# Second mixer's input projection: every weight block in the 512-column form, halves joined by ScalarE and VectorE

## Chip, cores and metric

The kernel runs on one core of one Trainium2 chip. The metric is the device time of one execution in microseconds (us), here the median of three runs.

## What is computed

A trunk of two layers over 256 tokens of width 2048, all in float32. Layer 0 mixes tokens with a gated linear recurrence, layer 1 with a state-space mixer (Mamba-2 SSD). Both layers then have a SwiGLU block and a gated per-layer embedding. The change lies in layer 1's mixer, cut here to its core:

```python
def ssd_mixer(u, w_in, conv_w, conv_b, dt_bias, a_log, d_skip, norm_g, w_out):
    zxbcdt = u @ w_in                       # 2048 -> 4096 (z) + 6144 (x, B, C) + 64 (dt)
    xbc = silu(causal_dwconv(xbc, conv_w, conv_b))      # 4 taps along the tokens
    xs, Bm, Cm = ...                        # 64 heads of 64; 8 groups share B and C of 128
    dt = softplus(dt + dt_bias)
    y = ssd_scan(xs, dt, -exp(a_log), Bm, Cm) + d_skip * xs
    y = y * silu(z)
    return (rmsnorm_per_group(y) * norm_g) @ w_out
```

## The kernel before

Activations lie transposed, 128 channels by 256 tokens a tile. To get float32 accuracy from a rounded format, each weight block and each activation tile is split into a high part (rounded) and a low part (the rest). A product of a 128x128 weight block is high x high + high x low + low x high. There are two forms of it (`piece`, lines 405 to 422). The three-matmul form (lines 401 to 403) adds all three products of 256 columns onto one half of a PSUM bank. The 512-column form does high weight x (high and low activations) in one matmul of 512 columns over the whole bank (line 419), then low weight x high activations over its first half (line 421). The result is then the sum of the two halves, which somebody has to add. `WIDE` (line 55) names the phases that use the 512-column form.

Weights come in pieces of eight blocks (512 KB) through a ring of four. SyncE loads piece p+4 when VectorE has finished the low part of piece p (`w_lo`). ScalarE rounds a landed piece to its high part (line 631, `w_hi`) when TensorE has used up the piece four before (`w_used`), VectorE subtracts to get the low part (line 925, `w_lo`), TensorE waits for `w_lo`. In their streams, ScalarE and VectorE handle piece q+3 first in step q, then the other work of step q.

The input projection of the mixer is phase B1. It runs in two halves of four head groups; between and after them comes the output projection B2. A head group makes ten output tiles from 20 pieces, two pieces a tile, in banks 2, 3, 0, 1 in turn: tiles 0 to 5 (B, C and four x tiles) go through the convolution, tiles 6 to 9 are z. Steps 0 to 11 use the three-matmul form and steps 12 to 19 the other, since z tiles are multiplied for a SiLU only. In odd steps VectorE waits for the piece and empties the bank: `bank x rinv` into `cpad` (line 1325), or for z tiles a reduce over both halves (`fold`, line 1123) and a multiply by half of rinv (line 1331). In even steps ScalarE does the tap of weight 3 with the bias (line 859), VectorE the other three (`later_taps`, lines 1133 and 1135), each waiting for the one before, ScalarE the Tanh of the tile before (line 866) and VectorE its SiLU (line 1318). Tile 5's Tanh and SiLU come in step 13.

After piece 14 TensorE needs all six SiLUs (`silu_done`): it multiplies B with C (line 568, 572) and transposes the x tiles (line 576). State products follow after piece 16 (line 582), outputs after pieces 17 and 19 (lines 594, 596). ScalarE makes the decay factors with Relu and Exp (lines 883, 887) in steps 11, 13, 15 and 17. Steps 0 to 8 also finish the head group before: its y on VectorE in step 0, a statistics matmul after piece 4 (line 603), variance and reciprocal in step 5 (lines 1390, 1391), the norm in step 7 (line 1396). In the very first head group there is none before, but the decay sums of all heads are computed in these steps (`decay_steps`), and their rows are read back by a DMA on SyncE's queue ahead of later weight loads. 

Of the kernel before, what the change touches and what calls it, by code (L numbers as in the profile page):

```python
# [54 lines left out]
WIDE = ("A2", "F1", "F2", "B2")  # L55
# [67 lines left out]
def trunk(nc, t, out):  # L123
    with ExitStack() as ctx:
# [73 lines left out]
        wdt = scratch(HEADS)  # L198

# [43 lines left out]
        eb_in, carry_mm, y_done_state = sem("eb_in"), sem("carry_mm"), sem("y_done_state")  # L243
        turned, xdec_done = sem("turned"), sem("xdec_done")
# [154 lines left out]
        def _(pe):  # L399
# [5 lines left out]
            def piece(ph, it, q, blocks):  # L405
# [3 lines left out]
                for b, (before, dst, src, k, first, last) in enumerate(blocks):  # L409
# [4 lines left out]
                    if ph["name"] not in WIDE and not (ph["name"] == "B1" and q >= 12 or gate):  # L414
                        mm = three(dst[:, 0:SEQ], whi[:, q % RING, cols], wlo[:, q % RING, cols], src[:, 0, k, :],
                                   src[:, 1, k, :], first, last)
                        continue
# [201 lines left out]
        def _(act):  # L619
# [38 lines left out]
            for index, ph in enumerate(phases):  # L658
# [97 lines left out]
                def body(it, first, ph=ph, name=name, n=n, index=index):  # L756
                    last = isinstance(it, int) and it == ph["iters"] - 1
                    for q in range(n):
# [84 lines left out]
                        if name == "B1":  # L843
                            group = it + ph["half"] * 4
                            very_first = first and ph["half"] == 0
                            if very_first:
# [70 lines left out]
        def _(dve):  # L917
# [139 lines left out]
            for index, ph in enumerate(phases):  # L1057
# [110 lines left out]
                def body(it, first, ph=ph, name=name, n=n, index=index):  # L1168
                    last = isinstance(it, int) and it == ph["iters"] - 1
                    for q in range(n):  # L1170
                        p = it * n + ph["piece0"] + q
                        w = width_of(index, ph, q, last)
                        if w and not (first and index == 0 and q == 0):
# [122 lines left out]
                        if name == "B1":  # L1296
# [12 lines left out]
                            if q % 2 == 0 and 2 <= q <= 12:  # L1309
                                nt = q // 2 - 1  # L1310
                                dve.wait_ge(tap_done, group * 6 + nt + 1)
                                later_taps(cpad[:, nt % 2], ca[:, nt, :],
                                           lambda k, nt=nt, group=group: flat(bpar[:, at(group), nt * 5 + k:nt * 5 + k + 1]),
                                           conv_done)
                            if q % 2 == 0 and 4 <= q <= 12 or q == 13:
                                nt = (q + 1) // 2 - 2
                                dve.wait_ge(conv_t, group * 6 + nt + 1)
                                V.scalar_tensor_tensor(out=ca[:, nt, :], in0=cth[:, nt % 2, :], scalar=1.0,
                                                       in1=ca[:, nt, :], op0=ALU.add, op1=ALU.mult).then_inc(silu_done, 1)
                            if q % 2 == 1:  # L1320
                                dve.wait_ge(w_used, p + 1)
                                src = bank[BANKS4[q // 2 % 4]][:, 0:SEQ]
                            if q % 2 == 1 and q < 12:
                                nt = q // 2
                                V.tensor_tensor(cpad[:, nt % 2, 3:3 + SEQ], src, rinv[:], ALU.mult).then_inc(bank_free, 1)
# [269 lines left out]
```

## Time and profile before

| | |
|---|---|
| median of 3 runs | 2690.71 us |
| lowest, highest | 2690.18, 2691.59 us |
| profiled execution | 2691.32 us |
| its span, first to last instruction | 2689.6 us |
| mean granted TensorE clock | 0.998 |
| TensorE busy | 99% |
| VectorE busy | 75% |
| ScalarE busy | 51% |
| GpSimd busy | 11% |

Shares are of the span. A busy TensorE isn't one at its peak, since matmuls overlap; the time from one start to another counts. Phase B1 lies between 1152 and 1412 us (first half) and between 1502 and 1751 us (second half), B2 behind each.

### The profile page before, as it was taken

To read this page: it belongs to the slowest core of one execution; us is meant where nothing else is said; L and a number is where in the kernel's file an instruction comes from. 1 tells how busy PE (TensorE), PEld (TensorE's weight loads), DVE (VectorE), ACT (ScalarE), POOL (GpSimd) and SP (SyncE) were. 2 spreads that over 40 slices of the span, in tenths; PEclk is the share of its full clock that TensorE was granted. 3 is DMA by queue.
4 is the path that set the end of the run, shared out by engine and by line. 5 is a ranking of instruction groups with operands and counts; after the bars stand their busy time and mean duration, and the time that the engine had idled before them with its cause. 6 is when DMAs were issued, how large, how long until landed. Compare 5 with 4: busy or idle time off the path is not lost.

```text
span 2689.6 us, 47811 instructions
## 1 busy us (share of the span) xinstructions
PE 2665.1 (99%) x16831; PEld 2400.6 (89%) x16831; DVE 2004.4 (75%) x2805; ACT 1377.1 (51%) x1869; POOL 284.9 (11%) x314
## 2 busy tenths in 40 slices
PE   9999999999999999999999999999999999999998
PEld 8999888888888888899998999988888888888887
DVE  7788776665666677889996799978666556667776
ACT  6776444444444445556664566644444444444454
POOL 1001300000000111100001000032000000001211
PEclk9999999999999999999999999999999999999999
DMA  6545565556655566655555555555555665555664
GB/s 217 179 173 193 178 199 187 188 174 189 206 189 188 192 189 197 191 178 185 190 185 187 202 183 188 188 186 189 187 189 179 184 206 190 191 189 173 188 202 137
DMA packets 154237, 504.62 MB, mean 188 GB/s; under 512 B 17104, under 2 KB 21520, under 8 KB 152976
## 3 DMA queue, kind: packets, MB, share of 16 engines
q1 hardware_dynamic: 154048, 503.14, 57.8%
q8 instruction: 64, 1.05, 0.2%
q14 instruction: 45, 0.37, 0.0%
q10 hardware_dynamic: 80, 0.07, 0.0%
HBM read 500.97 MB, written 2.16 MB: 187 GB/s over the span
## 4 chain that ended last, share of the span: by engine, by line
PE 95%; DVE 3%; ACT 1%; DMA 1%; issue 1%; SPq 0%; DVEq 0%; ACTq 0%
PE bank L419 51%; PE bank L421 26%; PE bank L401 5%; PE bank L403 5%; PE bank L402 5%; DVE wlo L925 1%; ACT whi L631 0%; PE bank L594 0%; DMA wraw<-in_A 0%; PE bank L576 0%; PE bank L582 0%; PE bank L596 0%; DMA wraw<-in_B 0%; DVE arena L1133 0%; DVE rinvh L979 0%
## 5 line engine op out<-in xcount | busy, mean ns | idle before, releaser
L419 PE MATMUL bank<-R,whi 128*128 128x512 f32 x5984 | 2089.0, 393 | 0.1
L421 PE MATMUL bank<-R,wlo 128*128 128x256 f32 x5984 | 1675.1, 280 | 0.0
L925 DVE TENSOR_TENSOR wlo<-wraw,whi 128x1024 fp32r<-128x1024 f32 (+2 forms) x1008 | 1166.5, 1164 | 545.8 <-ACT whi L631 544.0
L631 ACT ACTIVATE whi<-wraw 128x1024 fp32r<-128x1024 f32 (+2 forms) x1008 | 984.3, 983 | 917.6 <-PE bank L421 831.1
L419 PEld LDWEIGHTS bank<-R,whi 128*128 128x128 f32 x5984 | 1121.0, 187 | 252.5 <-issue 1.7
L421 PEld LDWEIGHTS bank<-R,wlo 128*128 128x128 f32 x5984 | 1130.8, 189 | 0.1
L401 PE MATMUL bank<-R,whi 128*128 128x256 f32 x1376 | 393.0, 286 | 5.1 <-DVE wlo L925 5.0
L403 PE MATMUL bank<-R,wlo 128*128 128x256 f32 x1376 | 389.5, 283 | 0.0
L402 PE MATMUL bank<-R,whi 128*128 128x256 f32 x1376 | 389.3, 283 | 0.0
L401 PEld LDWEIGHTS bank<-R,whi 128*128 128x128 f32 x1376 | 262.4, 191 | 9.6 <-DVE wlo L925 4.9
L402 PEld LDWEIGHTS bank<-R,whi 128*128 128x128 f32 x1376 | 262.5, 191 | 0.2
L403 PEld LDWEIGHTS bank<-R,wlo 128*128 128x128 f32 x1376 | 262.5, 191 | 0.0
L1123 DVE TENSOR_REDUCE arena<-bank 128x256 f32<-128x512 f32 x238 | 164.1, 690 | 57.5 <-PE bank L421 55.3
L1455 POOL TENSOR_TENSOR R<-arena,R 128x256 f32 x88 | 76.9, 874 | 1145.4 <-ACT R L830 1145.4
L830 ACT ACTIVATE R<-arena 128x256 f32 (+1 forms) x88 | 36.8, 418 | 187.1 <-DVE arena L1276 187.1
L1436 POOL TENSOR_TENSOR square<-h 128x256 f32 (+1 forms) x65 | 43.6, 670 | 485.8 <-DVE h L1249 481.3
L1437 POOL TENSOR_TENSOR sumsq<-sumsq,square 128x256 f32<-128x256 f32 x65 | 72.5, 1115 | 5.1
L1133 DVE SCALAR_TENSOR_TENSOR arena<-arena,bpar 128x256 f32<-128x256 f32 x96 | 53.2, 554 | 9.3 <-ACT arena L859 4.9
L1463 POOL TENSOR_TENSOR arena<-arena 128x512 f32<-128x512 f32 x8 | 10.9, 1364 | 454.0 <-ACT arena L898 454.0
L1248 DVE TENSOR_TENSOR h<-bank,h 128x256 f32<-128x256 f32 (+1 forms) x112 | 47.3, 423 | 8.6 <-PE bank L421 8.0
L1249 DVE TENSOR_TENSOR h<-bank,h 128x256 f32<-128x256 f32 (+1 forms) x112 | 47.6, 425 | 3.9
L971 DVE SCALAR_TENSOR_TENSOR R<-h,gains,R 128x256 fp32r<-128x256 f32 (+1 forms) x80 | 46.6, 582 | 3.2 <-DVE R L961 2.5
(177 smaller groups left out, 1274.9 us busy)
## 6 DMA issues: line engine op xcount, KB each, us to landing
wraw<-in_F SPq DMA_DIRECT2D x352, 512.0 KB, 3.3
wraw<-in_B SPq DMA_DIRECT2D x224, 512.0 KB, 3.3
wraw<-in_A SPq DMA_DIRECT2D x96, 512.0 KB, 3.6
wraw<-in_F SPq DMA_DIRECT2D x128, 384.0 KB, 3.1
wraw<-in_F SPq DMA_DIRECT2D x128, 320.0 KB, 3.2
wraw<-in_PL SPq DMA_DIRECT2D x64, 512.0 KB, 3.7
arena<-cs_rows SPq DMA_DIRECT2D x8, 1024.0 KB, 5.5
arena<-in_gates SPq DMA_DIRECT2D x8, 512.0 KB, 3.7
```

Source lines behind the costliest of these rows:

```text
L401: nc.tensor.matmul(dst, hi_w, hi_x, start=first, stop=False)
L402: nc.tensor.matmul(dst, hi_w, lo_x, start=False, stop=False)
L403: return nc.tensor.matmul(dst, lo_w, hi_x, start=False, stop=last)
L419: nc.tensor.matmul(dst.rearrange("p (s t) -> p s t", s=2), whi[:, q % RING, cols], src[:, :, k, :], start=first, stop=False)
L421: mm = nc.tensor.matmul(dst[:, 0:SEQ], wlo[:, q % RING, cols], src[:, 0, k, :], start=False, stop=last)
L631: nc.scalar.activation(whi[:, slot, 0:w * BLOCK], wraw[:, slot, 0:w * BLOCK], ACT.Copy).then_inc(w_hi, 1)
L925: V.tensor_tensor(wlo[:, slot, 0:w * BLOCK], wraw[:, slot, 0:w * BLOCK], whi[:, slot, 0:w * BLOCK].bitcast(F32), ALU.subtract).then_inc(w_ ...
L1123: own.link(V.tensor_reduce(dst, bank[number][:].rearrange("p (s t) -> p t s", s=2), mybir.AxisListType.X, ALU.add))
L1133: own.link(V.scalar_tensor_tensor(out=dst, in0=pad[:, k:k + SEQ], scalar=taps(k), in1=dst, op0=ALU.mult, op1=ALU.add))
L1249: V.tensor_tensor(row, src[:, SEQ:2 * SEQ], row, ALU.add).then_inc(bank_free, 1)
L1437: G.tensor_tensor(sumsq[:], sumsq[:], square[:], ALU.add).then_inc(sumsq_done, 1)
L1455: G.tensor_tensor(flat(dst[:, 1, at(it * 2 + j), :]), swi_u[:, j, :], flat(dst[:, 0, at(it * 2 + j), :]).bitcast(F32), ALU.subtract).then_ ...
```

## The change

`"B1"` joins `WIDE`, so that all 20 pieces of a head group use the 512-column form. In each odd step ScalarE copies the second half of the bank into a new two-buffer tile `low_half` (`half_done`), and VectorE adds it to the first half into the tile's place, then multiplies in place by rinv (or half of it) and frees the bank. The reduce isn't used in B1 any more. The taps are spread: in an even step VectorE does taps 2 and 1 of a tile with the SiLU of the tile before between them; its last tap comes in the next odd step, between the add and the multiply of the next tile. Tile 5's SiLU moves from step 13 to the very start of step 14, ahead of the weights' low part; its Tanh stays in step 13. VectorE's own count per head group goes from 26 to 32.

```diff
--- before.py
+++ after.py
@@ -52,7 +52,7 @@
 LAST_HEAD = {0: (0, 1), 1: (2, 3), 2: (4,), 3: (5,), 4: (6,), 5: (7,)}
 
 
-WIDE = ("A2", "F1", "F2", "B2")
+WIDE = ("A2", "B1", "F1", "F2", "B2")
 LAST = ((0, 4), (4, 4), (8, 4), (12, 2), (14, 2))
 GELU_C = 0.7978845608028654
 GELU_S = 0.044715 ** 0.5
@@ -196,6 +196,7 @@
         cst = scratch(2 * HEADS).rearrange("p (c e) -> p c e", c=2)
         dtt = scratch(2 * HEADS).rearrange("p (c e) -> p c e", c=2)
         wdt = scratch(HEADS)
+        low_half = scratch(2 * SEQ).rearrange("p (n t) -> p n t", n=2)
 
         dt_x, dt_e, dt_w, dt_z = [xtok[0:HEADS, c, n * SEQ:(n + 1) * SEQ] for c in range(2) for n in range(2)]
         dt_r, dt_v, dt_cs, dt_one = [zt[0:HEADS, n, :] for n in range(4)]
@@ -241,6 +242,7 @@
         tap_done, conv_done, conv_t, silu_done = sem("tap_done"), sem("conv_done"), sem("conv_t"), sem("silu_done")
         z_t, ebc_done, exp_done, sc_done = sem("z_t"), sem("ebc_done"), sem("exp_done"), sem("sc_done")
         eb_in, carry_mm, y_done_state = sem("eb_in"), sem("carry_mm"), sem("y_done_state")
+        half_done = sem("half_done")
         turned, xdec_done = sem("turned"), sem("xdec_done")
         y_mm, y_read, ysq_done, gstat_mm, gvar_done, grinv_done = (sem("y_mm"), sem("y_read"), sem("ysq_done"),
                                                                    sem("gstat_mm"), sem("gvar_done"), sem("grinv_done"))
@@ -411,7 +413,7 @@
                         pe.wait_ge(s, v)
                     cols = slice(b * BLOCK, (b + 1) * BLOCK)
                     gate = ph["name"] == "PL" and k < KT and not (q > 37 or q == 37 and b > 1)
-                    if ph["name"] not in WIDE and not (ph["name"] == "B1" and q >= 12 or gate):
+                    if ph["name"] not in WIDE and not gate:
                         mm = three(dst[:, 0:SEQ], whi[:, q % RING, cols], wlo[:, q % RING, cols], src[:, 0, k, :],
                                    src[:, 1, k, :], first, last)
                         continue
@@ -843,6 +845,11 @@
                         if name == "B1":
                             group = it + ph["half"] * 4
                             very_first = first and ph["half"] == 0
+                            if q % 2 == 1:
+                                act.wait_ge(w_used, p + 1)
+                                act.wait_ge(bank_free, it * 10 + ph["group0"] + 4 + q // 2 - 1)
+                                nc.scalar.activation(low_half[:, q // 2 % 2, :], bank[BANKS4[q // 2 % 4]][:, SEQ:2 * SEQ],
+                                                     ACT.Copy).then_inc(half_done, 1)
                             if very_first:
                                 decay_steps(q)
                             if q == 0 and not first:
@@ -1170,6 +1177,8 @@
                     for q in range(n):
                         p = it * n + ph["piece0"] + q
                         w = width_of(index, ph, q, last)
+                        if name == "B1" and q == 14:
+                            conv_silu(it + ph["half"] * 4, 5)
                         if w and not (first and index == 0 and q == 0):
                             lo(p + LEAD, q + LEAD, w)
                         g0 = it * ph["groups"] + ph["group0"] + 4
@@ -1309,26 +1318,24 @@
                             if q % 2 == 0 and 2 <= q <= 12:
                                 nt = q // 2 - 1
                                 dve.wait_ge(tap_done, group * 6 + nt + 1)
-                                later_taps(cpad[:, nt % 2], ca[:, nt, :],
-                                           lambda k, nt=nt, group=group: flat(bpar[:, at(group), nt * 5 + k:nt * 5 + k + 1]),
-                                           conv_done)
-                            if q % 2 == 0 and 4 <= q <= 12 or q == 13:
-                                nt = (q + 1) // 2 - 2
-                                dve.wait_ge(conv_t, group * 6 + nt + 1)
-                                V.scalar_tensor_tensor(out=ca[:, nt, :], in0=cth[:, nt % 2, :], scalar=1.0,
-                                                       in1=ca[:, nt, :], op0=ALU.add, op1=ALU.mult).then_inc(silu_done, 1)
+                                second = tap(group, nt, 2)
+                                if nt:
+                                    conv_silu(group, nt - 1)
+                                own.need(second)
+                                third = tap(group, nt, 1)
                             if q % 2 == 1:
-                                dve.wait_ge(w_used, p + 1)
-                                src = bank[BANKS4[q // 2 % 4]][:, 0:SEQ]
-                            if q % 2 == 1 and q < 12:
-                                nt = q // 2
-                                V.tensor_tensor(cpad[:, nt % 2, 3:3 + SEQ], src, rinv[:], ALU.mult).then_inc(bank_free, 1)
-                            if q % 2 == 1 and q > 12:
-                                j = q // 2 - 6
-                                if j == 0 and not very_first:
+                                tile = q // 2
+                                dst = cpad[:, tile % 2, 3:3 + SEQ] if tile < 6 else zt[:, tile - 6, :]
+                                dve.wait_ge(half_done, group * 10 + tile + 1)
+                                if tile == 6 and not very_first:
                                     dve.wait_ge(yn_lo, group * 4)
-                                fold(BANKS4[q // 2 % 4], zt[:, j, :])
-                                V.tensor_tensor(zt[:, j, :], zt[:, j, :], rinvh[:], ALU.mult).then_inc(bank_free, 1)
+                                folded = own.mark(V.tensor_tensor(dst, bank[BANKS4[tile % 4]][:, 0:SEQ], low_half[:, tile % 2, :],
+                                                                  ALU.add))
+                                if 1 <= tile <= 6:
+                                    own.need(third)
+                                    last_tap(group, tile - 1)
+                                own.need(folded)
+                                V.tensor_tensor(dst, dst, rinv[:] if tile < 6 else rinvh[:], ALU.mult).then_inc(bank_free, 1)
                             if q in (14, 16, 18):
                                 z_silu(group, q // 2 - 7)
                             if q == 18:
@@ -1365,6 +1372,23 @@
                                                 cbm.rearrange("p c l -> p (c l)").rearrange("p (e n) -> p e n", e=1)
                                                 .broadcast_to([P, 4, SEQ]), ALU.mult).then_inc(sc_done, 1)
 
+                def weight_of(group, nt, k):
+                    return flat(bpar[:, at(group), nt * 5 + k:nt * 5 + k + 1])
+
+                def tap(group, nt, k):
+                    return own.mark(V.scalar_tensor_tensor(out=ca[:, nt, :], in0=cpad[:, nt % 2, k:k + SEQ],
+                                                           scalar=weight_of(group, nt, k), in1=ca[:, nt, :],
+                                                           op0=ALU.mult, op1=ALU.add))
+
+                def last_tap(group, nt):
+                    V.scalar_tensor_tensor(out=ca[:, nt, :], in0=cpad[:, nt % 2, 0:SEQ], scalar=weight_of(group, nt, 0),
+                                           in1=ca[:, nt, :], op0=ALU.mult, op1=ALU.add).then_inc(conv_done, 1)
+
+                def conv_silu(group, nt):
+                    dve.wait_ge(conv_t, group * 6 + nt + 1)
+                    V.scalar_tensor_tensor(out=ca[:, nt, :], in0=cth[:, nt % 2, :], scalar=1.0,
+                                           in1=ca[:, nt, :], op0=ALU.add, op1=ALU.mult).then_inc(silu_done, 1)
+
                 def z_silu(group, j):
                     dve.wait_ge(z_t, group * 4 + j + 1)
                     own.mark(V.scalar_tensor_tensor(out=zt[:, j, :], in0=cth[:, j % 2, :], scalar=1.0,
@@ -1396,7 +1420,7 @@
                         V.scalar_tensor_tensor(out=zt[:, j, :], in0=zt[:, j, :], scalar=flat(bpar[:, at(group), 34 + j:35 + j]),
                                                in1=grms[:], op0=ALU.mult, op1=ALU.mult).then_inc(yn_done, 1)
 
-                steps(dve, ph, body, own, {"A1": 14, "B1": 26, "F1": 6, "PL": 0, "F2": 4}.get(name, 8))
+                steps(dve, ph, body, own, {"A1": 14, "B1": 32, "F1": 6, "PL": 0, "F2": 4}.get(name, 8))
                 own.close()
             dve.wait_ge(h_done, 2 * KT)
             V.tensor_tensor(swi_u[:, 0, :], h[:, KT - 1, :], h[:, KT - 1, :], ALU.mult).then_inc(last_square, 1)
```

## Rows read from the trace of the kernel before

**Rows 1.** The page: busy time of each engine; the chain that ended last.

```profile
PE 2665.1 (99%) x16831; PEld 2400.6 (89%) x16831; DVE 2004.4 (75%) x2805; ACT 1377.1 (51%) x1869; POOL 284.9 (11%) x314
...
PE 95%; DVE 3%; ACT 1%; DMA 1%; issue 1%; SPq 0%; DVEq 0%; ACTq 0%
```

**Rows 2.** Windows, line 401: window, length, PE busy (x), PEld busy (x), clock, DMA share, GB/s.

```profile
1349.99:1364.47 14.48, 11.41 (x40) 7.66 (x40) 1.00 0.45 152
1364.74:1385.06 20.32, 16.03 (x56) 10.52 (x56) 1.00 0.62 221
```

**Rows 3.** Windows, line 419: behind the three-matmul form; first 32 blocks of B2; its rest.

```profile
1385.08:1393.54 8.46, 8.46 (x24) 4.38 (x24) 1.00 0.69 220
1412.41:1423.79 11.38, 11.38 (x32) 6.00 (x32) 1.00 0.43 152
1424.06:1501.88 77.82, 77.82 (x224) 41.96 (x224) 1.00 0.58 192
```

**Rows 4.** Windows, one steady head group: PE, PEld, DVE, ACT, POOL busy, clock, DMA.

```profile
1350.00:1412.40 62.40, 62.40 (x473) 58.70 (x473) 57.12 (x86) 40.38 (x66) 6.28 (x6) 1.00 0.56 189
```

**Rows 5.** Timeline of VectorE, steps 9 to 13: start, duration, what, idle before.

```profile
1382.71 0.42 DVE L1325 TENSOR_TENSOR arena<-bank,rinv 128x256 f32<-128x256 f32 x1
1383.04 1.22 DVE L925 TENSOR_TENSOR wlo<-wraw,whi 128x1024 fp32r<-128x1024 f32 x1
1384.17 1.00 DVE L1133 SCALAR_TENSOR_TENSOR arena<-arena,bpar 128x256 f32<-128x256 f32 x2
1385.21 0.49 DVE L1135 SCALAR_TENSOR_TENSOR arena<-arena,bpar 128x256 f32<-128x256 f32 x1
1385.61 0.42 DVE L1318 SCALAR_TENSOR_TENSOR arena<-arena 128x256 f32<-128x256 f32 x1
...
1391.89 0.42 DVE L1318 SCALAR_TENSOR_TENSOR arena<-arena 128x256 f32<-128x256 f32 x1
```

**Rows 6.** Timeline of ScalarE, the same stretch.

```profile
1384.92 1.26 ACT L883 ACTIVATE arena<-arena 128x128 f32<-128x128 f32 x4
1386.22 0.63 ACT L887 ACTIVATE arena<-arena 128x512 f32<-128x512 f32 x1
...
1390.53 0.42 ACT L866 ACTIVATE arena<-arena 128x256 f32<-128x256 f32 x1 [0.98 <-DVE arena L1135]
```

**Rows 7.** Groups by line and form: busy us, mean ns, idle before.

```profile
L1248 DVE TENSOR_TENSOR h<-bank,h 128x256 f32<-128x256 f32 x80 | 33.7, 422 | 8.0 <-PE bank L421 8.0
...
L709 ACT ACTIVATE arena<-bank,apar 128x256 f32<-128x256 f32 x32 | 12.6, 476 | 0.1
```

**Rows 8.** Timeline of TensorE behind piece 14, the same head group.

```profile
1393.55 0.61 PE L568 MATMUL bank<-arena 128*128 128x128 f32 x4
...
1394.21 1.04 PE L576 MATMUL bank<-ident,arena 128*128 128x128 f32 x8
1395.01 0.47 PE L419 MATMUL bank<-R,whi 128*128 128x512 f32 x1
```

**Rows 9.** Timelines, second half's first head group: its start, last SiLU, line 568.

```profile
1501.89 0.28 PE L401 MATMUL bank<-R,whi 128*128 128x256 f32 x1
...
1541.84 0.42 DVE L1318 SCALAR_TENSOR_TENSOR arena<-arena 128x256 f32<-128x256 f32 x1
...
1544.93 0.27 PE L568 MATMUL bank<-arena 128*128 128x128 f32 x1
```

**Rows 10.** Timelines of ScalarE, VectorE and TensorE, the very first head group.

```profile
1195.60 1.06 ACT L631 ACTIVATE whi<-wraw 128x1024 fp32r<-128x1024 f32 x1 [2.29 <-DMA wraw<-in_B]
...
1204.05 0.42 DVE L1318 SCALAR_TENSOR_TENSOR arena<-arena 128x256 f32<-128x256 f32 x1
...
1204.52 0.71 PE L568 MATMUL bank<-arena 128*128 128x128 f32 x4 [2.31 <-DVE arena L1318]
```

**Rows 11.** Windows around that wait, all engines; the clock stands behind POOL's.

```profile
1202.22:1205.66 3.44, 1.14 (x10) 1.14 (x11) 3.27 (x6) 2.93 (x7) 0.00 (x0) 1.00 0.58 173
1205.66:1209.07 3.41, 3.41 (x15) 3.02 (x13) 3.11 (x6) 3.28 (x8) 0.00 (x0) 0.50 0.47 155
```

## Prediction

> **What bounds the kernel now.** I read the page's busy and chain lines first: TensorE is busy 99% of the span and holds 95% of the chain that ended last [rows 1]. So a cheaper product shortens the run, unless another engine then makes TensorE wait. Next come the windows by line, which give the time of one 128x128 weight block in either form. The three-matmul form takes 20.34 us for 56 blocks, 363 ns each, its first block after another matrix included; apart from that it runs at 360 ns [rows 2]. (The windows are cut 0.01 us inside the starts they lie between, so the stretch is 0.02 us longer than its row says.) The 512-column form has two paces: 8.48 us for 24 blocks (353 ns) right behind the three-matmul form, and 77.84 us for 224 blocks (347.5 ns) once a statistics matmul (line 603) has come between [rows 3]. Both forms move 768 columns, so the gain is small per block: 7 or 13 ns. Last I read VectorE and ScalarE beside it. In one steady head group of 62.4 us VectorE is busy 57.1 us [rows 4]; it is off the chain, but with little to spare.
>
> **TensorE's saving.** The change touches 12 of 20 pieces, 96 blocks, in each of 8 head groups. In a steady one (all but the first of each half):
> - Pieces 0 to 4, 40 blocks: now 14.50 us [rows 2]. The output projection starts behind the same matmuls and takes 11.40 us for 32 wide blocks, 356 ns each with the first block's delay [rows 3]; 8 more at 354 ns make 14.23. Saving 0.27 us.
> - Pieces 5 to 11, 56 blocks behind the statistics: now 20.34 us. At 347.5 ns 19.46, and I add 0.14 for the slow first block: 19.60. Saving 0.74 us.
> - Pieces 12 to 14, 24 blocks: now 8.48 us behind the three-matmul form, later at the faster pace 8.32. Saving 0.15 us.
>
> That is 1.16 us, and TensorE would reach the B and C products (line 568) at 1393.55 - 1.16 = 1392.39 instead of 1393.55 [rows 8]. The first head group of the second half has no statistics matmul and comes from the fast pace: 120 blocks at 347 ns take 41.6 us where 43.04 now lie between 1501.89 (96 blocks of 360 ns, 24 of 353) and 1544.93 [rows 9]: 1.4 us. In all 6 x 1.16 + 1.4 = 8.4 us, if nothing waits.
>
> One rule of the Trainium skill speaks against even that. "TensorE: Matmul & The Clock Gate", Back-to-back issue gap, gives a warm matmul its columns over 2.4 GHz plus 2.5 ns; a block saves one matmul and so 2.5 ns, an estimate of 1.9 us for 768 blocks. The trace disagrees (360 against 347 to 353 ns) and I go by the trace.
>
> **What VectorE and ScalarE pay.** Each conv tile today: one multiply out of the bank, which holds VectorE 0.33 us (1382.71 to 1383.04), three taps 1.44 us (1384.17 to 1385.61) and the SiLU 0.34 [rows 5]. After the change: an add and a multiply, 0.33 each, three taps that no longer wait for each other, 0.41 each (1385.21 to 1385.61 shows that spacing), the SiLU 0.34. That is 2.24 against 2.11, so 0.13 to 0.16 us more per tile. The four z tiles get cheaper (an add over 256 columns for a reduce over 512), but they come later. No row shows an add of a bank half with the saved half; the nearest is the add of a bank half onto h, 0.42 us, and ScalarE's nearest read of a bank half is 0.48 us [rows 7]. I take 0.42 for both; 0.35 to 0.50 moves the sum below by 0.15 us a head group. ScalarE does ten such copies a head group, and each waits for the end of its own piece, one piece later than what ScalarE does there now. Queued behind the copy of piece 11 are four Relus (1.27 us) and an Exp (0.63 us) [rows 6] and only then the next weight rounding, on which VectorE's subtraction of weights waits. TensorE has 2 us and more of weights in hand there, so I cost that at nothing for the weights; it eats 0.2 to 0.5 us of VectorE's time.
>
> **Where it hurts.** The chain that matters is the one to line 568, which needs the SiLU of all six conv tiles. Today the last tap of tile 5 is done in step 12 and its SiLU ends at 1391.89 + 0.42 = 1392.31 [rows 5], 1.24 us before TensorE arrives at 1393.55 [rows 8]. The change puts the last tap of a tile behind the fold of the next one, and the last SiLU into step 14. VectorE comes to that fold (tile 6) when it comes to the last SiLU today, plus three tiles' extra 0.16: 1391.89 + 0.48 = 1392.37. Then: add 0.34, last tap 0.48, hand over 0.04, Tanh on ScalarE 0.42 [rows 6], hand over 0.04, SiLU 0.42, hand over 0.04: 1394.15. TensorE waits for it from 1392.39: a wait of 1.76 us, where there was none. The head group's end moves by 1394.15 - 1393.55 = +0.60 us, and TensorE's 1.16 us is swallowed. Bounds: the extra work of the three tiles hidden in VectorE's pauses and cheap copies give +0.0; a late ScalarE gives +1.1. Six such head groups: +3.6 us (0 to +6.6).
>
> Second half's first head group: VectorE isn't behind there, its last SiLU ends at 1542.26, 2.67 us before line 568 [rows 9]. The new chain starts at the end of piece 13. Copy, add, tap, Tanh and SiLU with their handovers take 2.5 us against 2.77 of piece 14, and the late rounding behind the Relus costs some 0.7 us: TensorE waits 0.4 us. Net -1.4 + 0.4 = -1.0 us (-1.4 to -0.4).
>
> Very first head group: VectorE also computes the decays there and TensorE already waits 2.31 us for the SiLU; ScalarE waits 2.29 us for a weight piece whose load stands behind the decay rows' [rows 10]. TensorE's saving is worth nothing. The decay sums, and with them that load, come some 0.9 us later by three tiles' extra work and unhidden waits between an add and its multiply; behind it the copies, the last tap behind the fold, and ScalarE's order cost another 1.1: +2.0 us. After such a wait the granted clock is seen at 0.50 for 3.41 us and had been 1.00 in the 3.44 us before [rows 11]; it fell while products and transposes ran. A wait twice as long keeps it low for as long or for up to twice that, 0 to +1.7 us; I take +0.9. Together +2.9 us (+1 to +5).
>
> **Sum.** +3.6 - 1.0 + 2.9 = +5.5 us. The profiled execution took 2691.32 us (span 2689.6 and 1.7 around it), 0.6 above the median, so 2696.8 for it and 2696.2 for the median of 2690.71. A measurement of this kernel can tell about 0.2%, 5.4 us, from no change; the forecast lies on that edge.
>
> **Rivals.**
> - *The SiLU chain is in time* (faster). If VectorE reaches the tile-6 fold before piece 13 ends, the chain of 2.5 us fits inside piece 14 and every saving stays. Speaks for it: the taps' mutual waits go, and the last SiLU stands ahead of the weights in step 14. Against: VectorE's 57.1 of 62.4 us and hardly a pause between 1382 and 1392 [rows 4, 5]. It decides at a wait under 1.16 us at line 568: below that the head group is faster. With none: -8.4 and +2.9 for the very first, 2685.2 us; from there down to 2682.3 if the first costs nothing.
> - *The clock falls in every steady head group* (slower still). The new wait of 1.76 us is followed by 1.46 us of B/C products and transposes (1393.55 to 1395.01) [rows 8]. In the first head group the engine waited 2.31 us [rows 10] and was in its products and transposes when the clock fell [rows 11]. Its 3.41 us at 0.50 (1.2 of 2.4 GHz) cost half of themselves, 1.7 us. Six times that: 2706.4 us. The Trainium skill says in "TensorE: Matmul & The Clock Gate", Part 4: PE-mode transpose, that transposes don't count as busy for the gate; this trace agrees (it fell during them), and with the rule this rival would be the likelier for it. Against it stands that the steady wait is shorter than the first head group's 2.31.
> - *The change moves nothing* because the slower of two engines sets the head group anyway: the wait comes out near 1.16 us, -0.3 to +0.3 each, and the second half's first -1.0 and the very first's +2.9 stay: 2692.6 us.
>
> **How the numbers follow.** Forecast (waits of 1.2 to 2.3 us) 0.50; chain in time 0.20; clock falls too 0.14; nothing moves 0.16. The range 2684 to 2706 takes in most of the fast rival and the edge of the clock one. Faster by over 0.2% comes from most of the first rival and a little else: 0.18. Slower by over 0.2%: somewhat over half of the forecast's, all of the clock's, little else: 0.44. Within: 0.38.
>
> **What the profile will show.** In steady head groups: line 568's group waits some 1.8 us for the SiLU's line on VectorE; the pace is 354 ns before the statistics matmul and 347 after; VectorE's add for tile 6 starts later than TensorE's piece 13 ended; VectorE shows ten adds and no reduces in this phase. The prediction is wrong if line 568 waits under a microsecond in steady head groups, if a weight piece is waited for outside the first, or if the granted clock is under 1 there.

## The result

The changed kernel takes 2701.23 us (median of 7 runs, 2700.01 to 2703.08); the kernel before took 2690.71 us beside it (2688.57 to 2693.5). The ratio is 1.0039, 95% interval 1.0030 to 1.0048: slower by 0.39%, 10.5 us. The forecast was 2696.2 us with 2684 to 2706 as its range, and slower by over 0.2% was the likeliest class. So the sign and the place were right, and the size was about half of the real one. In the profiled pair the span went from 2689.6 to 2698.8 us, +9.2; that is less than 10.5 because the profiled execution before took 0.6 us more than its median and the one after, 2700.46 us, 0.8 us less than its own.

The page of the changed kernel, busy and chain lines, to be held against [rows 1]:

```profile
PE 2661.7 (99%) x16063; PEld 2361.0 (87%) x16063; DVE 2001.5 (74%) x2853; ACT 1396.3 (52%) x1949; POOL 289.3 (11%) x314
...
PE 85%; DVE 7%; ACT 4%; issue 3%; DMA 1%; SPq 0%; DVEq 0%; ACTq 0%
```

TensorE has 768 matmuls fewer and is busy 3 us less, as the change means it. But its share of the chain that ended last fell from 95% to 85%. VectorE holds 7% of it, ScalarE 4%. A kernel that was bound by TensorE now hands its end to two other engines in between. (These shares say where the chain runs and not what that costs: the time grew by 0.39%.)

Where they take over is seen at line 570 (568 before), the B/C products behind piece 14. This is TensorE's timeline in a steady head group of the changed kernel (start us, duration, what, idle before and who ended it):

```profile
1332.21 0.28 PE L423 MATMUL bank<-R,wlo 128*128 128x256 f32 x1
1334.30 0.71 PE L570 MATMUL bank<-arena 128*128 128x128 f32 x4 [1.80 <-DVE arena L1389]
1334.84 0.39 PE L574 MATMUL bank<-arena 128*128 128x128 f32 x2
1335.06 1.04 PE L578 MATMUL bank<-ident,arena 128*128 128x128 f32 x8
1335.86 0.47 PE L421 MATMUL bank<-R,whi 128*128 128x512 f32 x1
```

The last matmul of piece 14 starts at 1332.21 and the next one could start 0.12 us later, at 1332.33. It starts at 1334.30: a wait of 1.97 us counted from start to start (waits below are counted like that; the view counts idle time from the modelled end of the matmul, so it says 1.80). In [rows 8] there is no wait at this place. Line 1389 is VectorE's SiLU. Its chain, on VectorE and ScalarE:

```profile
1329.04 1.23 DVE L932 TENSOR_TENSOR wlo<-wraw,whi 128x1024 fp32r<-128x1024 f32 x1 [0.66 <-ACT whi L633]
1330.18 0.48 DVE L1379 SCALAR_TENSOR_TENSOR arena<-arena,bpar 128x256 f32<-128x256 f32 x1
1330.57 0.42 DVE L1389 SCALAR_TENSOR_TENSOR arena<-arena 128x256 f32<-128x256 f32 x1
1330.91 0.48 DVE L1379 SCALAR_TENSOR_TENSOR arena<-arena,bpar 128x256 f32<-128x256 f32 x1
1331.31 1.22 DVE L932 TENSOR_TENSOR wlo<-wraw,whi 128x1024 fp32r<-128x1024 f32 x1
1332.44 0.42 DVE L1332 TENSOR_TENSOR arena<-bank,arena 128x256 f32<-128x256 f32 x1
1332.77 0.48 DVE L1384 SCALAR_TENSOR_TENSOR arena<-arena,bpar 128x256 f32<-128x256 f32 x1
1333.17 0.42 DVE L1338 TENSOR_TENSOR arena<-arena,rinvh 128x256 f32<-128x256 f32 x1
1333.73 0.43 DVE L1389 SCALAR_TENSOR_TENSOR arena<-arena 128x256 f32<-128x256 f32 x1
```

```profile
1330.66 0.36 ACT L851 ACTIVATE arena<-bank 128x256 f32<-128x256 f32 x1
1333.29 0.42 ACT L873 ACTIVATE arena<-arena 128x256 f32<-128x256 f32 x1 [2.27 <-DVE arena L1384]
```

From top to bottom: the weights' low part (line 932) that had to wait 0.66 us for ScalarE, tap, SiLU of tile 4, tap, the next low part, and only now the fold of tile 6 (line 1332), behind it the deferred last tap of tile 5 (line 1384), the Tanh on ScalarE (line 873) and the last SiLU. When VectorE begins that fold, TensorE is already standing. ScalarE's half copy for it (line 851) had been ready for 1.4 us.

The second part of the loss is in the clock. Windows of the changed kernel (all engines' busy time, then the granted clock, DMA share, GB/s):

```profile
1205.85:1209.26 3.41, 3.41 (x15) 3.41 (x16) 1.15 (x2) 3.38 (x7) 0.00 (x0) 0.50 0.33 120
1612.03:1615.44 3.41, 3.41 (x16) 3.12 (x14) 1.99 (x4) 2.64 (x4) 0.00 (x0) 0.50 0.10 34
1676.88:1680.29 3.41, 3.41 (x16) 3.22 (x15) 1.87 (x4) 2.76 (x4) 0.00 (x0) 0.50 0.11 40
```

The first is the fall that [rows 11] shows too. The other two are new: in two of the six steady head groups the clock goes to 1.2 GHz for 3.41 us, 0.7 to 0.8 us behind the end of the wait. The head group starts that bound these stretches, and the B/C products in them:

```profile
1226.57 0.50 PE L421 MATMUL bank<-R,whi 128*128 128x512 f32 x1
1270.93 0.37 PE L570 MATMUL bank<-arena 128*128 128x128 f32 x1 [1.80 <-DVE arena L1389]
...
1416.53 0.50 PE L421 MATMUL bank<-R,whi 128*128 128x512 f32 x1
1547.89 0.38 PE L570 MATMUL bank<-arena 128*128 128x128 f32 x1
1566.85 0.50 PE L421 MATMUL bank<-R,whi 128*128 128x512 f32 x1
1611.22 0.37 PE L570 MATMUL bank<-arena 128*128 128x128 f32 x1 [1.81 <-DVE arena L1389]
1676.20 0.37 PE L570 MATMUL bank<-arena 128*128 128x128 f32 x1 [1.80 <-DVE arena L1389]
...
1759.99 0.50 PE L421 MATMUL bank<-R,whi 128*128 128x512 f32 x1
```

Against the same starts of the kernel before (1225.15, 1412.40, 1563.78 and 1751.04) the account of the 9.2 us is:

| stretch | before | after | change |
|---|---|---|---|
| up to the second head group | 1225.15 | 1226.57 | +1.42 |
| three steady head groups, first half | 187.25 | 189.96 | +2.71 |
| output projection and second half's first head group | 151.38 | 150.32 | -1.06 |
| three steady head groups, second half | 187.26 | 193.14 | +5.88 |

Phase B1 starts within 0.1 us of the same time in both profiles, so the first row is the very first head group. A steady head group without a fall of the clock takes 0.9 us more (2.71 / 3). The two with a fall make the last stretch 5.88 - 2.71 = 3.2 us longer than the first half's, 1.6 us each.

### The profile page after: what moved, and what is told of

It reads as the page before. It is cut to its first block, busy times and chain, and to the rows that moved or that the text cites. A ratio compares the mean times of both kernels' runs of the same rounds, so it can differ in the third digit from the quotient of the medians.

```text
span 2698.8 us, 46563 instructions
## 1 busy us (share of the span) xinstructions
PE 2661.7 (99%) x16063; PEld 2361.0 (87%) x16063; DVE 2001.5 (74%) x2853; ACT 1396.3 (52%) x1949; POOL 289.3 (11%) x314
## 4 chain that ended last, share of the span: by engine, by line
PE 85%; DVE 7%; ACT 4%; issue 3%; DMA 1%; SPq 0%; DVEq 0%; ACTq 0%
PE bank L421 51%; PE bank L423 27%; DVE wlo L932 2%; PE bank L403 2%; PE bank L405 2%; PE bank L404 2%; ACT whi L633 1%; DVE arena L1379 0%; DVE arena L1338 0%; DVE arena L1332 0%; DVE arena L1420 0%; DMA wraw<-in_A 0%; PE bank L578 0%; ACT arena L890 0%; PE bank L596 0%
## 5 line engine op out<-in xcount | busy, mean ns | idle before, releaser
L421 PE MATMUL bank<-R,whi 128*128 128x512 f32 x6752 | 2359.4, 394 | 0.6 <-DVE wlo L932 0.6
L421 PEld LDWEIGHTS bank<-R,whi 128*128 128x128 f32 x6752 | 1265.4, 187 | 288.0 <-issue 2.6
L403 PE MATMUL bank<-R,whi 128*128 128x256 f32 x608 | 173.7, 286 | 4.9 <-DVE wlo L932 4.7
L1130 DVE TENSOR_REDUCE arena<-bank 128x256 f32<-128x512 f32 x206 | 142.1, 690 | 48.2 <-PE bank L423 45.9
L404 PE MATMUL bank<-R,whi 128*128 128x256 f32 x608 | 171.9, 283 | 0.0
L403 PEld LDWEIGHTS bank<-R,whi 128*128 128x128 f32 x608 | 116.2, 191 | 7.9 <-DVE wlo L932 4.9
L404 PEld LDWEIGHTS bank<-R,whi 128*128 128x128 f32 x608 | 116.3, 191 | 0.1
L851 ACT ACTIVATE arena<-bank 128x256 f32<-128x256 f32 x80 | 30.1, 376 | 81.2 <-PE bank L423 81.2
L1487 POOL TENSOR_TENSOR arena<-arena 128x512 f32<-128x512 f32 x8 | 11.3, 1413 | 468.7 <-ACT arena L905 468.7
```

What stands on the lines that cost most here:

```text
L403: nc.tensor.matmul(dst, hi_w, hi_x, start=first, stop=False)
L404: nc.tensor.matmul(dst, hi_w, lo_x, start=False, stop=False)
L421: nc.tensor.matmul(dst.rearrange("p (s t) -> p s t", s=2), whi[:, q % RING, cols], src[:, :, k, :], start=first, stop=False)
L1130: own.link(V.tensor_reduce(dst, bank[number][:].rearrange("p (s t) -> p t s", s=2), mybir.AxisListType.X, ALU.add))
```

## The experiments

Times are medians beside runs of the kernel before on the same chip, which were 2690.7, 2691.1 and 2691.6 us in the three sets. Waits are at the B/C products in steady head groups; where two of a half agree and the third is a little less, the common value stands.

### The form alone

```diff
-WIDE = ("A2", "F1", "F2", "B2")
+WIDE = ("A2", "B1", "F1", "F2", "B2")
```

VectorE's and ScalarE's programs are those of the kernel before, so the second half of the bank is left out of the conv tiles: this version shows the time of the form and nothing else.

> The kernel before with B1 in the 512-column form and nothing else changed; the second half of the bank is not added for the conv tiles, so its output lacks that term. Theory (the form saves 8.4 us on TensorE, and VectorE's chain to line 568 has 1.24 us to spare in a steady head group, which takes the 1.16 saved): no wait at the B/C products in steady head groups, TensorE reaches them 1.1 to 1.2 us earlier, time 2682 to 2684 us. Rival (the form itself is worth nothing, or its pace in a loop over head groups is no better): 2689 to 2692 us.

Measured: 2682.68 us, ratio 0.997 (0.9958 to 0.9982), no wait in any steady head group. B/C products at 1328.32 and 1389.58, 61.26 us apart where the kernel before needs 62.42:

```profile
1327.62 0.41 DVE L1318 SCALAR_TENSOR_TENSOR arena<-arena 128x256 f32<-128x256 f32 x1
```

```profile
1328.32 0.38 PE L568 MATMUL bank<-arena 128*128 128x128 f32 x2
```

The first line is VectorE's last SiLU, the second TensorE's product: the SiLU ends at 1328.03, 0.29 us ahead. Before it was 1.24 us ahead; TensorE has used up most of that room. So the form is worth about what was worked out from the two paces: 8.1 us by the medians (4.8 to 11.3 by the interval) for 8.4. In the trace the seven head groups for which the 8.4 us were forecast are 8.0 us shorter (1.16 each in the first half's three, 1.07 in the second's, 1.3 in the second half's first with the output projection ahead of it). The very first adds 0.5 us that was not forecast: its B/C products come 1.18 us later, but the clock doesn't fall behind them. VectorE has 0.29 us left to give. By the rule of the Trainium skill that the prediction weighed ("TensorE: Matmul & The Clock Gate", Back-to-back issue gap), which the page gives for the isolated gap of a matmul, it would have been an estimate of 1.9 us; the measurement decides against it for these matmuls.

### The spread taps alone

On the kernel before, in its old form and with its old evacuation:

```diff
 even step:
-    later_taps(...)            # taps 2, 1, 0, each waiting for the one before
-    silu(nt - 1)
+    tap 2; silu(nt - 1); tap 1
 odd step, behind the evacuation of the next tile:
+    last tap of the tile before
-step 13: silu(5)
+step 14, ahead of the weights' low part: silu(5)
```

> The kernel before with only the taps spread as in the change (last tap behind the next tile's evacuation, last SiLU at the start of step 14); form and evacuation as before. Theory (the deferred tap costs some 1.7 us of chain but only the faster form and the slower evacuation turn that into a wait): a wait of 0 to 0.5 us at the B/C products in steady head groups, time 2690 to 2694 us. Rival (the spread taps alone are the loss): wait above 1.5 us, 2699 to 2702 us.

Measured: 2691.70 us, ratio 1.0005 (0.9996 to 1.0014), a wait of 0.05 to 0.08 us. The later SiLU costs all of the 1.24 us of room, and hardly more. Neither the form nor the spread taps make the loss alone; each uses the same room. The form with the spread taps but without the adds and half copies was not run, so how the loss divides between the later hand-over and VectorE's extra work isn't shown by this pair.

### Tile 5 early

On the changed kernel:

```diff
 step 12, VectorE:
     third = tap(group, nt, 1)
+    if nt == 5: own.need(third); last_tap(group, 5)
 step 13, ScalarE:
+    Tanh of tile 5
     half copy of tile 6
-    Tanh of tile 5
 VectorE:
-step 14, first: conv_silu(5)
+step 13, first: conv_silu(5)
```

> The changed kernel, but tile 5's last tap stays in step 12, its Tanh comes ahead of the half copy in step 13 and its SiLU at the start of step 13. Theory (the wait is the chain add, last tap, Tanh, SiLU behind the fold of tile 6): the SiLU ends some 1.3 us earlier, the wait of 1.97 us in a steady head group falls to 0.4 to 0.8, the granted clock stays at 1.00 in all of them, time 2687 to 2692 us. Rival (VectorE's and ScalarE's added work is the loss, wherever the last tap stands): wait about 2 us, 2699 to 2702 us.

Measured: 2688.16 us, ratio 0.9990 (0.9981 to 0.9999); the wait falls from 1.97 to 0.72 us, the clock stays at 1.00 in all steady head groups. One tile's last tap, Tanh and SiLU, each moved ahead by at most one step, are worth 13 us, with no less work for any engine. In the profiled pair the six steady head groups are 10.7 us shorter: 7.5 from the shorter waits, 3.2 from the two falls of the clock that are gone. So the chain behind the fold of tile 6 is what TensorE waited for.

### All taps back

On the changed kernel all three taps of a tile are in the even step again, each waiting for the one before, and the last SiLU is behind the low part of step 13. The adds and half copies stay.

> The changed kernel with all three taps back in the even step, each waiting for the one before, and the last SiLU in step 13 behind the weights' low part (its Tanh ahead of the half copy). The adds and half copies stay. Theory as a chain of VectorE's work (each tile costs some 0.3 us more without the spreading, so the SiLU ends no earlier than in the changed kernel): wait 1.8 to 2.8 us, 2700 to 2706 us. Rival (the spreading is the loss, all of it): wait under 0.5 us, 2685 to 2690 us.

Measured: 2699.55 us, ratio 1.0033 (1.0021 to 1.0045). Waits of 2.0 to 2.2 us in the first two steady head groups of each half and 1.2 to 1.3 us in the third, and the clock falls in three of the six. The time is half a microsecond under what the chain theory allowed; the wait is in its range but for the third head groups. The six executions spread from 2696.66 us (mean granted clock 0.997) to 2703.41 us (0.995), so how often the clock falls differs from one execution to the next. The loss is there without the spreading, so the spreading alone isn't the mistake: VectorE, which now adds as well and whose taps wait for each other again, is about as late as with it. What matters is when VectorE gets to the last SiLU, by its whole load and its order.

### The Relus of step 11 later

In step 11 of the changed kernel ScalarE copies the half bank of piece 11 and then does four Relus and an Exp before it rounds the next weights:

```profile
1324.91 1.05 ACT L633 ACTIVATE whi<-wraw 128x1024 fp32r<-128x1024 f32 x1
1325.86 0.36 ACT L851 ACTIVATE arena<-bank 128x256 f32<-128x256 f32 x1
1326.12 1.27 ACT L890 ACTIVATE arena<-arena 128x128 f32<-128x128 f32 x4
1327.42 0.63 ACT L894 ACTIVATE arena<-arena 128x512 f32<-128x512 f32 x1
1327.96 1.04 ACT L633 ACTIVATE whi<-wraw 128x1024 fp32r<-128x1024 f32 x1
```

There is no idle time before the copy (line 851): its wait for piece 11 costs nothing here. What stands between the two roundings is the copy's own 0.26 us and the 1.84 us of Relus and Exp. Here these come in step 13, behind the half copy and ahead of that step's own (shortened; the waits in front of the first block move with it):

```diff
-if q in (11, 13, 15, 17):
-    e0 = q - 11
+for e0 in {13: (0, 2), 15: (4,), 17: (6,)}.get(q, ()):
```

> The changed kernel with one move on ScalarE: the four Relus and the Exp of step 11 come in step 13 behind the half copy, so that the weight rounding behind them isn't held up by the wait for piece 11. Theory (the late rounding makes VectorE idle 0.66 us once in the chain to the last SiLU): the wait at the B/C products in a steady head group falls from 1.97 to 1.2 to 1.5 us, time 2694 to 2699 us depending on whether the clock still falls. Rival (ScalarE's order costs nothing, the chain is the deferred tap alone): wait stays at 1.9 to 2.0 us, 2700 to 2702 us.

Measured: 2694.49 us, ratio 1.0014 (1.0005 to 1.0023), wait 1.21 us in all six, the clock at 1.00 throughout B1, even in the very first head group. The 0.66 us that VectorE stood for `whi` in the timeline above is the second cause of the wait, and 1.97 - 1.21 = 0.76 us confirms it. But the steady head groups get only 0.23 us shorter each, because another wait has come up: two blocks of Relus now stand ahead of one rounding, VectorE waits 4.19 us for it behind the last SiLU, and TensorE waits some 0.4 us at the state products (line 584):

```profile
1334.68 1.22 DVE L931 TENSOR_TENSOR wlo<-wraw,whi 128x1024 fp32r<-128x1024 f32 x1 [4.19 <-ACT whi L633]
1338.25 0.60 PE L584 MATMUL bank<-arena 128*128 128x128 f32 x3 [0.18 <-DVE arena L1361]
```

Of the 7.5 us between the two profiled spans 1.4 come from the six steady head groups' waits, 3.2 from their two falls of the clock, and 2.7 from the very first head group, which has no fall either.

### Both

> Both moves: tile 5's tap and SiLU early, and the Relus of step 11 in step 13. Theory (the two causes add up): the wait falls from 0.72 to under 0.2 us, the head group comes down to 61.3 to 61.5 us, time 2683 to 2686 us. Rival (VectorE's extra add and multiply bind next, so the 0.72 us stays): 2687 to 2690 us.

Measured: 2686.05 us, ratio 0.9980 (0.9971 to 0.9989). The theory was half right: there is no wait at the B/C products any more, but a head group takes 62.15 us (61.95 in the third of a half) and not 61.4. The wait at the state products has grown to 0.5 to 0.7 us, seen in VectorE's timeline and TensorE's:

```profile
1270.65 1.23 DVE L934 TENSOR_TENSOR wlo<-wraw,whi 128x1024 fp32r<-128x1024 f32 x1 [2.52 <-ACT whi L633]
1271.79 0.42 DVE L1399 SCALAR_TENSOR_TENSOR arena<-arena 128x256 f32<-128x256 f32 x1
```

```profile
1274.23 0.94 PE L584 MATMUL bank<-arena 128*128 128x128 f32 x6 [0.45 <-DVE arena L1367]
```

Two blocks of Relus in step 13 hold up the next rounding, VectorE stands 2.52 us for it, and the decayed x tiles (line 1367), which stand behind it in VectorE's queue, come late for line 584.

### The decay rows' load behind a weight piece

Both moves, and in the very first head group SyncE issues piece 14's load ahead of the decay rows' loads, and ScalarE's Exp that reads the rows moves from step 11 to step 13.

> As before (both moves), and in the very first head group the loads of the decay rows stand behind the load of weight piece 14 instead of ahead of it, with the Exp that reads them in step 13. Theory (there the chain to the last SiLU begins with that weight load, for which ScalarE waits 1.9 us): the wait in the first head group falls by 1 to 2 us, time 2681 to 2684.5 us. Rival (VectorE's decay arithmetic sets that wait): no change against both moves alone.

Measured: 2687.38 us, ratio 0.9987 (0.9978 to 0.9996), no faster than both moves alone. The wait in the first head group isn't shorter but longer, 2.81 against 1.87 us, and the clock falls there, which it doesn't in the version with both moves. ScalarE's timeline says why:

```profile
1199.49 1.06 ACT L633 ACTIVATE whi<-wraw 128x1024 fp32r<-128x1024 f32 x1 [4.31 <-DMA wraw<-in_B]
```

ScalarE's wait for a load has gone from piece 14 (2.78 us in the version with both moves) to piece 15, which now stands behind the rows, and has grown to 4.31 us. Neither theory held: the wait moves with the load, but in this order the load hits the next piece. The Exp moved too, and what it does to the wait by itself wasn't tried.

### A reduce instead of the half copies

Tile 5 early, but VectorE sums both halves with one reduce over the bank, and ScalarE copies nothing.

> Tile 5 early, but the two halves are summed by VectorE's reduce over 512 columns straight from the bank; ScalarE's half copies are gone. Question: does ScalarE's help pay? Theory (VectorE is the one that is short of time; a reduce takes 0.69 us where the add takes 0.41): the wait grows from 0.72 to 1.1 to 1.6 us, time 2690 to 2696 us. Rival (the copies' waits on ScalarE cost as much as they save): 2686 to 2689 us.

Measured: 2689.05 us, ratio 0.9993 (0.9984 to 1.0002), wait 0.85 to 0.91 us in two head groups of each half, 0.3 to 0.4 in the third. Below the theory's range and next to the rival's: against the version with the copies (2688.16, wait 0.72) it can't be told from no change. The reduce costs VectorE 0.69 us where the add costs 0.41, but without the copies ScalarE's roundings come earlier: in a steady head group VectorE waits 0.8 us for them in all, with the copies 2.3 us. So ScalarE's help is nearly eaten by the roundings that it makes late. Whether the copies' own time or their waits for the pieces do that isn't shown; the copies of steps 9, 11 and 13 had no idle time before them.

### The blocks spread over steps 13 to 17

```diff
-for e0 in {13: (0, 2), 15: (4,), 17: (6,)}.get(q, ()):
+for e0 in {13: (0,), 14: (2,), 15: (4,), 17: (6,)}.get(q, ()):
```

Tile 5 is early here too.

> Tile 5 early, and ScalarE's four blocks of Relus and Exp in steps 13, 14, 15 and 17, the second of them behind the z Tanh of step 14, so that step 13 holds one block as it did. With two blocks in step 13 the rounding of the next weight piece came late, VectorE waited 2.5 us for it and TensorE waited 0.7 us at the state products (line 584) in every steady head group. Theory: that wait goes, none takes its place, the head group takes 61.3 to 61.5 us and the whole 2680 to 2684 us. Rival (VectorE is short of time by as much, the wait only moves again): 2685 to 2688 us.

Measured: 2681.24 us (2679.41 to 2684.26), ratio 0.9964 (0.9950 to 0.9977): 0.36% faster than the kernel before and 20 us under the changed one. TensorE's and VectorE's timelines at the same place as above:

```profile
1324.63 0.28 PE L423 MATMUL bank<-R,wlo 128*128 128x256 f32 x1
1324.75 0.68 PE L570 MATMUL bank<-arena 128*128 128x128 f32 x4
```

```profile
1322.57 0.47 DVE L1384 SCALAR_TENSOR_TENSOR arena<-arena,bpar 128x256 f32<-128x256 f32 x1
1323.19 0.48 DVE L1389 SCALAR_TENSOR_TENSOR arena<-arena,bpar 128x256 f32<-128x256 f32 x1
1324.16 0.42 DVE L1394 SCALAR_TENSOR_TENSOR arena<-arena 128x256 f32<-128x256 f32 x1 [0.48 <-ACT arena L850]
1324.50 1.22 DVE L934 TENSOR_TENSOR wlo<-wraw,whi 128x1024 fp32r<-128x1024 f32 x1
1325.63 0.42 DVE L1337 TENSOR_TENSOR arena<-bank,arena 128x256 f32<-128x256 f32 x1
```

The product starts 0.12 us behind the last matmul. The last tap (line 1389 here) and SiLU (line 1394) come before the low part and the fold (line 1337), with 0.17 us to spare. Steady head groups take 61.26 to 61.37 us, as with the form alone (61.26 to 61.36), and the very first waits 1.17 us with no fall of the clock. So the rival, that VectorE is short of time and the wait only moves again, is ruled out: with all adds and copies in place only the order has changed.

### The clock by itself

Six products of no use on TensorE, between piece 14 and the wait, in the changed kernel (shortened: the second half's first head group has none):

```diff
+pe.wait_ge(silu_done, group * 6 + 4)
+for _ in range(6):
+    nc.tensor.matmul(bank[7] as 512 columns, R[1][:, 0, 0, 0:P], R[1][:, :, 0, :], start=True, stop=True)
 pe.wait_ge(silu_done, group * 6 + 6)
```

> The changed kernel with six 512-column products of no use on TensorE between piece 14 and the wait for the last SiLU (in all head groups but the second half's first), into a bank that is free there. They fill 1.3 us of a wait of 1.97 us and of 4.1 us. Theory (two falls of the granted clock in steady head groups and one in the first cost 1.6 to 1.7 us each, on top of the waits): the granted clock stays at 1.00 in the steady head groups, the last SiLU comes no later, time 2696.5 to 2699 us. Rival (the clock has no part in the loss): 2700 to 2702 us.

Measured: 2697.07 us (2695.94 to 2698.88), ratio 1.0020 (1.0011 to 1.0029).

```profile
1331.53 1.55 PE L568 MATMUL bank<-R 128*128 128x512 f32 x6
1333.49 0.71 PE L575 MATMUL bank<-arena 128*128 128x128 f32 x4 [0.41 <-DVE arena L1394]
```

The products end in a wait of 0.7 us instead of 1.97, the SiLU comes no earlier (a head group takes 63.3 us, as in the changed kernel where the clock held), and the granted clock is 1.00 everywhere but at the kernel's end, where it is low in every version. Doing useless work makes the kernel 4 us faster, and the two intervals (1.0011 to 1.0029, 1.0030 to 1.0048) don't overlap. That is about what the falls of the clock cost: three in the profiled execution of the changed kernel, 1.6 us each by the account above would be 4.8.

## Why the prediction was right, and where it was short

- **TensorE's saving** of 8.4 us: confirmed by the form alone, 8.1 us, and 8.0 in the trace at the places it was forecast for. The two paces of the 512-column form were read rightly; in the changed kernel a head group runs at 354 ns a block ahead of the statistics matmul and at 347 behind it.
- **The place.** The wait came at the B/C products, behind the SiLU of tile 5, by the chain written down: fold of tile 6, last tap, Tanh, SiLU. Weights were never what TensorE waited for in a steady head group.
- **The size of the steady wait** was 1.76 us by the sum and 1.97 in the trace. VectorE began the fold at 1332.44, 0.11 us behind TensorE's arrival at 1332.33, where the sum had it 0.02 ahead; and the chain from there took 1.86 us instead of 1.78, since TensorE started its product 0.14 us behind the SiLU's end instead of 0.04. The products themselves then took 0.1 us longer than in [rows 8]. A head group lost 0.9 us instead of 0.60: six times 0.3 is 1.8 us of the shortfall.
- **Luck in that size.** The sum has no term for ScalarE's late rounding: the prediction said that it eats 0.2 to 0.5 us of VectorE's time, but let it in only at the upper bound. With the Relus of step 11 moved away the wait is 1.21 us and not 1.76, and VectorE begins the fold at 1328.78, 0.64 us ahead of TensorE's arrival at 1329.42. So the sum put VectorE's other work some 0.6 us too late, left out a hold-up of 0.76 us, and the two errors hid each other.
- **The clock** was a rival with 0.14, all or nothing, at 1.7 us a head group. It was neither: two of six, at 1.6 us. Those 3.2 us are the largest part of the shortfall in the profiled pair. Here the step that failed was to ask whether the clock falls in a steady head group as one question with one answer, and so to put its cost at nothing in the sum. By the last of its own signs, a granted clock under 1 in steady head groups, the prediction is wrong in this point.
- **The second half's first head group**: -1.0 forecast, -1.06 measured, with a wait of 0.25 us for 0.4.
- **The very first head group**: +2.9 forecast, +1.42 measured. ScalarE's late weight piece came at 1195.98 against 1195.60, 0.4 us later and not 0.9, the B/C products 1.30 us later and not 2.0, and the low clock lasted 3.41 us as before, where 0.9 us more had been put in for it. After the wait of 4.12 us the clock was low once for 3.41 us; in the version with all taps back it was low for 6.83 us around a wait of 3.15 us, so "up to twice that" does occur. The 1.5 us too much here cancelled under a third of the 5.0 us that were missing in the steady head groups, which is luck too.
- **The half copy** took 0.38 us (0.36 above), the add 0.42; 0.42 had been taken for both.
- Put together: 6 x 0.9 + 3.2 - 1.06 + 1.42 = 9.0 of the span's 9.2 us.

The fast rival, that the chain is in time, needed a wait under 1.16 us. The version with tile 5 early shows it come true with another order, and the spread blocks at its full value. The third rival, that nothing moves, is ruled out by the result: the wait is 1.97 us and not near 1.16.

## What to carry to other kernels

Room on an engine that isn't the bound is spent once: the faster form on TensorE and the later hand-over on VectorE each used the same 1.24 us of room here with hardly a loss, and with both of them and the extra adds and copies the kernel lost 10 us. When work is interleaved in an in-order queue, keep the last item of a chain that another engine waits for out of the pattern; it has nothing behind it to overlap with. And move long blocks that nobody needs soon (the Relus and Exps) behind the urgent ones, one block a step: two in one step only moved the wait to the state products.

## What the runs showed of the hardware

- A wait's length alone doesn't decide whether the granted clock falls. In the changed kernel waits of the same 1.97 us were followed by a fall in two head groups and not in two others, while in the form alone TensorE waited 3.02 us in the very first head group and stayed at 1.00 (5.14 of the 8 us busy):

```profile
1202.00:1210.00 8.00, 5.14 (x35) 4.43 (x34) 7.45 (x15) 6.96 (x15) 0.00 (x0) 1.00 0.46 139
```

In the very first head group waits of 2.46, 2.53, 2.81, 3.01 and 4.12 us were followed by a fall in other versions, and waits of 2.38 and 2.68 us weren't. With all taps back the steady waits of 2.0 to 2.2 us were followed by a fall three times out of four. So a wait that recurs should be priced with a share of falls and not with all or none. What decides the single case isn't settled by these runs.
- Filling the wait with products kept the clock up, and no wait of 1.87 us or less was followed by a fall in any of the profiled executions. The Trainium skill says that transposes don't count as busy ("TensorE: Matmul & The Clock Gate", Part 4: PE-mode transpose). These runs don't decide that: of the eleven falls in B1 over all profiles three came while the transposes ran (one of them at 1612.03), seven while the products before them did (one at 1676.88) and one still in the wait, and the same products and transposes without a wait before them, as in [rows 8], were never followed by one.
- The pace of the 512-column form has a memory: 354 ns a block behind the three-matmul form or the output matmuls, 347 ns from the next statistics matmul on, for hundreds of blocks [rows 3]. Why wasn't tried.
